# Key-page matmuls as one block behind each projection slot instead of quarters inside it, in a one-core decoder step

## The reference, cut to what matters

```python
proj = h @ w_in                                   # (256 + 8 rows) x 1024 @ 1024 x 3072
past_k = cache_sb_k[layer][page_table].reshape(DEC_BATCH, n_pages * PAGE_SIZE, H_SB, HEAD_DIM)
k_all = jnp.concatenate([past_k, ka_s], axis=1)
z = jnp.einsum('bqhd,bkhd->bhqk', q, k).astype(jnp.float32) / math.sqrt(HEAD_DIM)
z = z + bias.astype(jnp.float32)[None, :, None, None]
```

## Time and profile before

| | us |
|---|---|
| median of three runs | 1240.13 |
| the profiled execution's own time | 1240.13 |
| its span (first to last instruction) | 1238.5 |
| PE busy, share of the span | 928.0, 75% |
| DMA queues 0 and 1, share of 16 engines | 72.0%, 25.0% |
| first key matmul starts | 99.84 |
| last key matmul ends | 207.25 |

### The profile page before, as it was taken

How to read it: one execution, slowest core, us unless ns; L and a number is a source line. 1 busy time by engine, 2 the same in 40 slices (tenths; PEclk the granted TensorE clock), 3 DMA queues, 4 the chain that set the end, 5 groups by cost and what they waited for, 6 DMA issues and landing times.

```text
span 1238.5 us, 14521 instructions
## 1 busy us (share of the span) xinstructions
PE 928.0 (75%) x3666; PEld 419.6 (34%) x3666; DVE 634.3 (51%) x1606; ACT 352.1 (28%) x959; POOL 442.1 (36%) x497
## 2 busy tenths in 40 slices
PE   2798994667676897994678778777777778777784
PEld 1343331345221245881223223333233323332231
DVE  3200101333555252502677777777777777777755
ACT  1000011344211201222333333233334443344333
POOL 2102333012354000111355545455444455544541
PEclk9898996678888998997899999999989999999986
DMA  9999999956799999999999999999989999999996
GB/s 366 421 395 383 389 413 386 401 234 247 247 383 380 306 337 349 402 386 388 409 427 421 427 427 428 427 428 428 427 369 427 427 427 427 427 427 423 428 427 271
DMA packets 83707, 481.20 MB, mean 389 GB/s; under 512 B 11881, under 2 KB 12234, under 8 KB 42322
## 3 DMA queue, kind: packets, MB, share of 16 engines
q0 software_dynamic: 57216, 366.03, 72.0%
q1 hardware_dynamic: 26450, 114.66, 25.0%
HBM read 477.40 MB, written 70.32 MB: 442 GB/s over the span
## 4 chain that ended last, share of the span: by engine, by line
DMA 38%; PE 33%; issue 11%; DVE 6%; ACT 6%; POOL 2%; POOLq 2%; SPq 1%; DVEq 0%; ACTq 0%
DMA R<-in_uv,idst 31%; PE ps L895 9%; PE ps L548 7%; PE ps L846 5%; DMA R<-in_sb_k 3%; PE ps L801 2%; PE ps L574 2%; POOL R L452 2%; DMA pages<-in_pages 1%; POOLq L285 1%; ACT wgt L1141 1%; DMA R<-in_wts 1%; DMA R<-in_sb_v 1%; DMA R<-in_uv,idec 1%; PE ps L516 1%
## 5 line engine op out<-in xcount | busy, mean ns | idle before, releaser
L895 PE MATMUL ps<-R,diag 128*128 128x512 f32 x1024 | 490.3, 628 | 162.8 <-ACT diag L1160 162.8
L452 POOL DMA_INDIRECT R<-in_uv,idst x256 | 313.3, 1224 | 358.6 <-PE ps L895 285.2
L1617 DVE CUSTOM_DVE_ANT_0 R<-R,H 128x1024 f32<-128x1024 f32 x264 | 319.3, 1223 | 193.9 <-DMA R<-in_uv,idst 182.7
L895 PEld LDWEIGHTS ps<-R,diag 128*128 128x128 f32 x1024 | 195.3, 199 | 457.8 <-ACT diag L1160 249.8
L1138 ACT ACTIVATE gel<-dots 128x2 f32<-128x2 f32 x132 | 26.8, 203 | 396.6 <-DVE dots L1617 396.6
L392 POOL DMA_DIRECT2D R<-in_wts x36 | 19.1, 530 | 243.9 <-PE ps L486 89.5
L548 PE MATMUL ps<-R,HT 128*128 128x512 f32 x192 | 93.3, 625 | 8.5 <-DMA R<-in_wts 8.5
L1160 ACT ACTIVATE diag<-const,wgt 128x128 f32<-128x128 f32 x256 | 88.8, 393 | 14.1 <-ACT wgt L1141 1.5
L676 PE MATMUL ps<-R,ast 128*32 128x512 f32 x256 | 56.1, 749 | 18.9 <-DMA R<-in_sb_v 17.9
L1141 ACT ACTIVATE wgt<-gel,gst 128x1 f32<-128x1 f32 x264 | 63.3, 287 | 4.3
L846 PE MATMUL ps<-HT,R 128*128 128x264 f32 x256 | 61.2, 400 | 0.7 <-ACT HT L926 0.7
(11 more groups left out here) (271 smaller groups left out, 839.7 us busy)
## 6 DMA issues: line engine op xcount, KB each, us to landing
R<-in_wts POOLq DMA_DIRECT2D x48, 1024.0 KB, 14.1
out_dil_k_s<-in_dil_k SPq DMA_DIRECT2D x32, 1023.5 KB, 8.4
out_dil_v_s<-in_dil_v SPq DMA_DIRECT2D x32, 1023.5 KB, 8.6
R<-in_sb_k SPq DMA_DIRECT2D x64, 256.0 KB, 7.9
R<-in_sb_k POOLq DMA_DIRECT2D x64, 256.0 KB, 6.2
R<-in_sb_v POOLq DMA_DIRECT2D x64, 256.0 KB, 5.5
R<-in_sb_v SPq DMA_DIRECT2D x64, 256.0 KB, 6.6
R<-in_uv,idst POOLq DMA_INDIRECT x256, 11.9
```

The lines of the kernel that those rows point to most:

```text
L452: pool.indirect_dma_start(out=R[:, row_slot(k), :], out_offset=None, in_=A["uv"], in_offset=bass.IndirectOffsetOnAxis(ap=idst[:, par, k:k ...
L895: last = pe.matmul(ps[:, banks + q, :], diag[:, k % 4, :], R[:, row_slot(k), D + q * 512:D + (q + 1) * 512], start=False, stop=False, skip ...
L1617: dve.tensor_tensor_reduce(u, u, H[:, t, :], 1.0, 0.0, ALU.mult, ALU.add, dots[:, k:k + 1]).then_inc(s["dot_done"], 1)
```

## The change

Only PE's program changes. `keys(b)` is no generator any more: its eight chunks are used in one go. It stands behind a slot, after the slot's `sample_rows` and so after `w_used`. Sample b comes one slot earlier than before: sample 0 behind slot (1, 1), sample 6 behind slot (2, 3), and sample 7 alone at the end. The matmuls, their operands and their number stay, as do all waits of the other engines and the order of all DMA requests on SP and POOL.

```diff
-            def qkv_slot(r, k, between=()):
-
-                parts = iter(between)
+            def qkv_slot(r, k):
+
                 w_round(r + 2, k)
...
                     if k == WSLOTS - 1:
                         last.then_inc(s["qkv_mm"], 1)
-                    next(parts, None)
...
                     last.then_inc(s["k_used"], 1)
-                    if cc % 2:
-                        yield
-
-            for k in range(WSLOTS):
-                qkv_slot(0, k)
-            qkv_slot(1, 0)
-            pe.wait_ge(s["qkv_ev"], 5)
-            turn_group(s4[:, 0, :], 5, 0, s["qz_mm"])
-            qkv_slot(1, 1)
-            pe.wait_ge(s["qz_ready"], 1)
-            for n in range(2, 2 * WSLOTS):
-                qkv_slot(1 + n // WSLOTS, n % WSLOTS, between=keys(n - 2))
-            for b in range(2 * WSLOTS - 2, NB):
-                for _ in keys(b):
-                    pass
+
+            for r in range(ROUNDS):
+                for k in range(WSLOTS):
+                    qkv_slot(r, k)
+                    if (r, k) == (1, 0):
+                        pe.wait_ge(s["qkv_ev"], 5)
+                        turn_group(s4[:, 0, :], 5, 0, s["qz_mm"])
+                    elif r > 0:
+                        if (r, k) == (1, 1):
+                            pe.wait_ge(s["qz_ready"], 1)
+                        keys((r - 1) * WSLOTS + k - 1)
+            keys(NB - 1)
```

## The result

The changed kernel takes 1255.74 us (median of 4 runs, 1253.91 to 1262.47) against 1240.26 us of the kernel before; the ratio is 1.0117, 95% interval 1.0088 to 1.0148 (the quotient of the two medians is 1.0125; below, the ratio counts). It is slower, outside the predicted range (1235.4 to 1244.0) and well past the 1239.7 forecast. Its profiled execution took 1252.58 us with a span of 1250.9.

The account below looks back on a forecast made before the run. Bound: the last key chunk's end, with PE and DMA level. Slot (1, 3)'s end 139.3 + 2.9 fixed + 63.5 transfer = 205.7, plus the last block 1.13: keys end 206.8 against 207.25, -0.4 us, 1239.7 us, range 1235.4 to 1244.0.

Parts of the forecast that it names:

- What bounds the stretch: 98 to 207 us: last key chunk's end, 207.25, shifts the program's end at full size; PE (12.5) and DMA (12.7) level.
- Sample 0 earlier: Keys at 97.9 to 101.9 us; POOL's odd requests for sample 1 from about 99.6 to 107.7, 2.6 to 4.4 earlier.
- Sample 1 before slot (1, 3): Sample 1 done at 129.5 us (128.2 to 130.8), then slot (1, 3) at a lower clock, ending at 139.3.
- The first dry window: During slot (1, 3) PE frees no chunk, so DMA idles about 3 us around 139.
- Five periods without a gap: From 139.3 us: 26.2 MB at 413 GB/s take 63.5 us with no further gap, last landing 205.7.
- Tail: Samples 6 and 7 together in about 19 us instead of 25.5; keys end at 206.8 against 207.25.
- The order of POOL's queue: Weight (2, 3) waits on POOL for slot (1, 3), sample 3's pages behind it; DMA idles about 3 us around 139.
- The clock: PE's lower clock after the long wait, in slot (1, 3): +1.7 us, 0 if the clock holds.
- Rival B: DMA runs dry once in each of five periods, PE freeing chunks in 4 of 12 us: +2.5 to +5 us; chance 0.26.

Follow-up runs that it names:

- e9: Changed kernel, still block, slot earlier and 8 buffers, with only POOL's weight requests moved along; 1245.05 us, ratio 1.0067 to the kernel before.
- e12: Repeat of e9: the changed kernel with 8 buffers and only POOL's weight requests moved along; 1246.07 us, ratio 1.0093 to the kernel before.
- e4: Changed kernel with 12 key chunk buffers in place of 8, PE's order and POOL's weights untouched; 1242.84 us, ratio 1.0030 to the kernel before.
- e7: Changed kernel with both 12 chunk buffers and POOL's weight requests moved along; 1237.78 us, ratio 1.0006 to the kernel before.
- e1: Kernel before with keys still in quarters inside a slot but one slot earlier, 8 buffers, POOL's weights as before; 1282.72 us, ratio 1.0337.

## Why the prediction was wrong, step by step

- *What bounds the stretch:* right. The end of the last key chunk sets everything behind it, and DMA and PE were level. The shift of 14.8 us at the keys came out as 12.4 us of span in the profiled pair and 15.5 us between the medians. Over all runs the time behind the keys was 1025 to 1036 us, so "at its full size" holds to 5 or 6 us, not exactly, and in e9 and e12 it fails: the keys are back and the time is not.
- *Sample 0 earlier:* the requests moved ahead by less, and bought nothing. POOL's odd requests went from 100.83 to 108.81 instead of 99.6 to 107.7, behind a weight that was requested at 99.04, and sample 1's first pair was used at 119.27, not before the 118.29 of the kernel before. The 1.3 us that the sum took off did not come.
- *Sample 1 before slot (1, 3):* the wait was 9.04 us (about 8 foretold), its end 131.6 (129.5, above the range's 130.8). The slot behind it ran at full clock, so it ended at 139.6 against the 139.3 foretold: two errors that cancel.
- *The first dry window:* right, about 3 us around 139 foretold, 3.3 us between 137.5 and 141.5 measured.
- *Five periods without a gap:* the step that failed. It said that requests of a block exceed 413 GB/s, and that "while PE does a slot (8.07 us) it still has the block to work off (4.19 MB, 10.2 us)". That is true only of a block used in one go, whose eight refills go out at its end. In a block that waits, PE frees each pair as it lands, the refills go out during the 10 us of the wait and are served during it. When PE takes up the slot at 161.34, only the last refills are still to come (the last odd one at 163.77). They are in by 168, the slot and its sample rows last until 171.5, and the first new bytes move behind 173. The next block is then fast, which makes its refills late and the block after it slow. So the loss returned in every second period: 11.9 us in three windows, where the sum had one of 3. The sum took a fast block's backlog for the steady state. From 139.56 the four slots and samples up to the end of slot (2, 3) took 62.7 us, until 202.25, where the prediction had that end near 187.5 to 190. Of the 15.3 us by which the keys' end was missed (222.06 against 206.8), the two windows that the sum lacked are 8.6; the rate also stood below 413 GB/s behind each dry window (284 GB/s from 141 to 144, 336 from 204 to 207), and the rest was not separated.
- *Tail:* right in size. Samples 6 and 7 took 19.8 us, about 19 foretold; the delay was there before they began.
- *The order of POOL's queue* was described, with the weight waiting on it, and was then counted only in the first gap. It belongs to the failed step: "no further gap" took the weight to be under way during the slot, and it stood there waiting for the slot's end (140.07, 171.83 and 202.76, each just behind a slot). At the end of the keys, moving the weights alone gives back 13.5 to 15.1 us of the 14.8 (e12, e9), the four buffers alone 11.5 (e4); they overlap, since either one fills the same windows. In the time, the weights give back only 0.2 to 0.5% of the 1.2%, the buffers 0.9%, both all of it (e7).
- *The clock:* taken at 1.7 us once, in slot (1, 3), where it did not come. It struck in two other slots (9.16 us at 161.34, 8.96 at 192.47, against 7.13), some 3.9 us of PE time. While such a slot lasts PE frees nothing, so it should lengthen the dry windows, but e7 has 3.15 us of the same and no loss. What it is worth within the 14.8 us was not separated.
- *Rival B* named the mechanism (DMA dry because PE frees chunks in bunches), at 0.26 and priced at 2.5 to 5 us, though its own likely ends, 209.5 to 211, make 2.3 to 3.8. Its price was 1.2 us a period in place of 4 us in every second one. It was discounted because a period's bytes (12.7 us) exceed PE's 12.1. That is an argument on the mean, and the loss is in the order of events within two periods.

The Trainium skill (DMA: Bandwidth & Descriptors, Rules for kernel authors) advises to issue a DMA early and to wait for it late. The rows agree on the half that I had treated as harmless: the change moved the waits ahead of the slot's compute, and with as many buffers as one sample has chunks a wait ahead of the compute is also a request held back behind it.

## What to carry to other kernels

Where loads and compute are level, look at what is outstanding when the longest stretch without a freed buffer begins, and compare it in us with that stretch; take it from a period that waits, not from one that does not. Free buffers evenly, or hold more than one stretch's worth of them. When a consumer's order moves, move each producer queue's order with it: a request that waits for the wrong slot holds back all that stands behind it, in e1 for some 40 us of the program. And a recovered end of a stage is not yet a recovered time: look at both.

## What was not expected of the hardware

With eight buffers and the weights in their old place the block settled in a rhythm of two periods, a full block of 3.64 us and a waiting one of about 10 us (151.08 to 161.34, 182.84 to 192.47), and held it to the end of the stretch. The recovery of DMA from nothing is short: in the changed kernel it stands at a share of 0.02 from 138 to 141 us and at 0.81 from 141 to 144, after the first request at 140.07:

```profile
138.00:141.00 3.00, 3.00 (x46) 1.46 (x48) 0.78 (x4) 0.98 (x2) 0.53 (x1) 1.00 0.02 10
141.00:144.00 3.00, 3.00 (x46) 1.53 (x35) 2.61 (x15) 0.00 (x0) 1.07 (x2) 1.00 0.81 284
```
